# An RWKV-7 core on one core: the triangular solver's levels for two chunks issued head by head in turn, the odd chunk on exchanged partition halves, removal keys ahead of the decays

## The reference, cut to what matters

```
def step(state, inp):
    r_t, w_t, k_t, v_t, kk_t, a_t = inp
    sa = jnp.einsum('bhvk,bhk->bhv', state, kk_t)
    state = (state * w_t[:, :, None, :]
             - sa[..., None] * (kk_t * a_t)[:, :, None, :]
             + v_t[..., None] * k_t[:, :, None, :])
    return state, jnp.einsum('bhvk,bhk->bhv', state, r_t)
```

## Time and profile before

| | us |
|---|---|
| median of 3 runs | 2342.1 (2340.4 to 2342.15) |
| time of the profiled execution | 2340.44 |
| its span, first to last instruction | 2338.4 |
| TensorE busy | 2235.1 (96% of the span) |
| VectorE busy | 1552.6 (66%) |
| ScalarE busy | 1210.3 (52%) |
| mean granted TensorE clock | 0.987 |

### The profile page before, as it was taken

How to read it: one execution, slowest core, us unless ns; L and a number is a source line. 1 busy time by engine, 2 the same in 40 slices (tenths; PEclk the granted TensorE clock), 3 DMA queues, 4 the chain that set the end, 5 groups by cost and what they waited for, 6 DMA issues and landing times. The chain is left out here.

```text
span 2338.4 us, 55662 instructions
## 1 busy us (share of the span) xinstructions
PE 2235.1 (96%) x23008; PEld 2146.5 (92%) x23008; DVE 1552.6 (66%) x2401; ACT 1210.3 (52%) x2061; POOL 35.9 (2%) x51
## 2 busy tenths in 40 slices
PE   6899899999999999999988998999999999999998
PEld 6799899999999988899977998999998999888998
DVE  7754465566665688665587644655776777876776
ACT  5643454455544456644466434544677444776443
POOL 0000000000000010000000000000100000100000
PEclk9899999999999999999998999999999999999999
DMA  5310255543455433355433102554433555434553
GB/s 201 126 47 4 71 191 188 173 144 118 154 196 188 153 118 119 126 201 191 156 99 127 47 4 85 187 188 168 148 116 129 180 197 171 136 118 142 191 184 112
DMA packets 88435, 327.14 MB, mean 140 GB/s; under 512 B 9808, under 2 KB 9936, under 8 KB 87632
## 3 DMA queue, kind: packets, MB, share of 16 engines
q1 hardware_dynamic: 87984, 322.66, 40.9%
q0 software_dynamic: 288, 2.10, 0.3%
HBM read 323.67 MB, written 1.05 MB: 139 GB/s over the span
## 5 line engine op out<-in xcount | busy, mean ns | idle before, releaser
L2050 PE MATMUL bank<-h_split,w_split 128*128 128x256 f32 x3176 | 913.4, 288 | 22.4 <-DVE h_split L2269 8.6
L2051 PE MATMUL bank<-h_split,w_split 128*128 128x256 f32 x3176 | 898.7, 283 | 0.0
L2052 PE MATMUL bank<-h_split,w_split 128*128 128x256 f32 x3176 | 898.4, 283 | 0.0
L2238 DVE TENSOR_TENSOR w_split<-ring_a,w_split 128x1024 fp32r<-128x1024 f32 x474 | 568.1, 1224 | 192.2 <-ACT w_split L2135 190.9
L2050 PEld LDWEIGHTS bank<-h_split,w_split 128*128 128x128 f32 x3176 | 604.0, 190 | 35.0 <-DVE h_split L2269 11.3
L2051 PEld LDWEIGHTS bank<-h_split,w_split 128*128 128x128 f32 x3176 | 599.2, 189 | 1.4
L2052 PEld LDWEIGHTS bank<-h_split,w_split 128*128 128x128 f32 x3176 | 598.1, 188 | 0.0
L2135 ACT ACTIVATE w_split<-ring_a 128x1024 fp32r<-128x1024 f32 x474 | 483.5, 1049 | 47.9 <-PE bank L594 25.8
L2072 PE MATMUL bank<-act_split,d_split 128*128 128x256 f32 x1008 | 285.4, 283 | 3.8 <-DVE act_last L2330 2.4
L2073 PE MATMUL bank<-act_split,d_split 128*128 128x256 f32 x1008 | 285.2, 283 | 0.0
L2074 PE MATMUL bank<-act_split,d_split 128*128 128x256 f32 x1008 | 285.1, 283 | 0.0
(11 more groups left out here) (282 smaller groups left out, 3235.6 us busy)
## 6 DMA issues: line engine op xcount, KB each, us to landing
ring_a<-wa SPq DMA_DIRECT2D x474, 512.0 KB, 4.0
ring_d<-wd SPq DMA_DIRECT2D x132, 512.0 KB, 4.5
tab_sb<-tab SPq DMA_DIRECT2D x1, 2384.0 KB, 13.3
hT<-na POOLq DMA_DIRECT2D x2, 1024.0 KB, 5.2
xT<-x SPq DMA_DIRECT2D x1, 1024.0 KB, 4.9
out<-xT SPq DMA_DIRECT2D x1, 1024.0 KB, 3.9
vec_sb<-vec SPq DMA_DIRECT2D x1, 288.0 KB, 4.9
tab_sb<-tab SPq DMA_DIRECT2D x1, 65.0 KB, 4.6
```

Of the source, the lines that this page charges most:

```text
L2050: mm(dst, w[:, 0, ks], x[:, 0, k, :], start=(k == 0), stop=False)
L2051: mm(dst, w[:, 0, ks], x[:, 1, k, :], start=False, stop=False)
L2052: last = mm(dst, w[:, 1, ks], x[:, 0, k, :], start=False, stop=(k == KT - 1))
L2238: v.tensor_tensor(w_split[:, u % 4, 1, :], ring_a[:, u % 4, :], w_split[:, u % 4, 0, :].bitcast(f32), ALU.subtract).then_inc(s["w_lo"], 1)
```

## The change

- **Levels in pairs.** `level_product`, `level_update` and `level_turned` now take two chunks at once and issue their heads in turn: head n of the even chunk, head n of the odd one. The odd chunk's `X`, `Q`, `XT` lie on the exchanged half: where the even chunk's product reads partitions 0 to 63 and writes 0 to 63, the odd chunk's reads 0 to 63 and writes 64 to 127. The right sides of the odd chunks are exchanged too, and `solve` turns the halves back.
- **The turned update** is now a transpose of the copied `X` by the identity, behind the product of the next level; the first one of an odd chunk (`turned_zero`) is a new operation and takes the place of a VectorE operation (1119) for that chunk. The last level (`last_turned`) is as before.
- **Scores of chunks 2 and 3** are cut into eight parts on banks 6 and 7, and two parts are issued in each level of chunks 0 and 1. The four `bonus_sum` come ahead of the levels.
- **Projections.** The removal keys come at units 16 and 17, ahead of the second half of the running sums, which moves from unit 15 to unit 18; the exponentials are split in two and come behind the evacuations; group 5 of the mixes comes a unit later; the low part of unit 21 comes behind group 5. In the second layer the value gates come between the products of line 1055.

```diff
+        def score_bank(c, i):
+            return level_bank(c, i % 3) if c < 2 else B[6 + i % 2]
...
+            def other(h):
+                return slice(HD, P) if h.start == 0 else slice(0, HD)
...
+            def turned_zero(c):
                 q, t = counts(c)
+                pe.wait_ge(s["q_ready1"], 6 * q + 1)
+                if c > 2:
+                    pe.wait_ge(s["xtn_ready1"], 6 * q)
+                b = eight(level_bank(c, 2)[:, :])
+                for n, h in each_head():
+                    last = mm(b[other(h), n, :], Xc[c][h, n, :], ident_of(h), start=True, stop=True)
+                last.then_inc(s["xt_mm1"], 1)
+            def level_product(a, lv):
+                q = counts(a)[0]
+                for t in range(2):
+                    if lv == 1:
+                        pe.wait_ge(s[f"q_ready{t}"], 6 * q + 1)
+                    else:
+                        pe.wait_ge(s[f"xn_ready{t}"], 4 * q + lv - 1)
+                b0, b1 = [eight(level_bank(a + t, 0)[:, :]) for t in range(2)]
+                for n, h in each_head():
+                    even = mm(b0[h, n, :], scb[a][h, n, CH:2 * CH], Xc[a][h, n, :], start=True, stop=True)
+                    odd = mm(b1[other(h), n, :], scb[a + 1][h, n, CH:2 * CH], Xc[a + 1][h, n, :], start=True, stop=True)
+                even.then_inc(s["lx_mm0"], 1)
+                odd.then_inc(s["lx_mm1"], 1)
+            def level_update(a, lv):
+                q = counts(a)[0]
+                for t in range(2):
+                    pe.wait_ge(s[f"q_ready{t}"], 6 * q + lv + 1)
+                if lv == 1:
+                    pe.wait_ge(s["xt_ready"], q + 1)
+                else:
+                    pe.wait_ge(s["xtn_ready0"], 5 * q + lv - 1)
+                pe.wait_ge(s["xtn_ready1"], 6 * q + lv)
+                b0, b1 = [eight(level_bank(a + t, 1)[:, :]) for t in range(2)]
+                for n, h in each_head():
+                    o = other(h)
+                    even = mm(b0[h, n, :], XTc[a][h, n, :], Qc[a][h, n, :], start=True, stop=True)
+                    odd = mm(b1[h, n, :], XTc[a + 1][o, n, :], Qc[a + 1][o, n, :], start=True, stop=True)
+                even.then_inc(s["xn_mm0"], 1)
+                odd.then_inc(s["xn_mm1"], 1)
+            def level_turned(a, lv):
+                q = counts(a)[0]
+                for t in range(2):
+                    pe.wait_ge(s[f"xn_ready{t}"], 4 * q + lv)
+                b0, b1 = [eight(level_bank(a + t, 2)[:, :]) for t in range(2)]
+                for n, h in each_head():
+                    even = mm(b0[h, n, :], Xc[a][h, n, :], ident_of(h), start=True, stop=True)
+                    odd = mm(b1[other(h), n, :], Xc[a + 1][h, n, :], ident_of(h), start=True, stop=True)
+                even.then_inc(s["xt_mm0"], 1)
+                odd.then_inc(s["xt_mm1"], 1)
+            def last_turned(c):
+                q, t = counts(c)
+                pe.wait_ge(s[f"q_ready{t}"], 6 * q + 6)
+                pe.wait_ge(s[f"xtn_ready{t}"], (5 + t) * q + 4 + t)
                 b = eight(level_bank(c, 2)[:, :])
                 for n, h in each_head():
                     last = mm(b[h, n, :], Qc[c][h, n, :], XTc[c][h, n, :], start=True, stop=True)
                 last.then_inc(s[f"xt_mm{t}"], 1)
...
                 pe.wait_ge(s["rhs_ready"], 4 * r + c + 1)
-                pe.wait_ge(s[f"xtn_ready{t}"], 5 * q + 5)
+                pe.wait_ge(s[f"xtn_ready{t}"], (5 + t) * (q + 1))
                 b = eight(chain_bank(c, "r")[:, :])
                 for n, h in each_head():
-                    last = mm(b[h, n, :], XTc[c][h, n, :], rhs_[h, n, :], start=True, stop=True)
+                    g = other(h) if c % 2 else h
+                    last = mm(b[h, n, :], XTc[c][g, n, :], rhs_[g, n, :], start=True, stop=True)
                 last.then_inc(s["u_mm"], 1)
...
-            level_product(1, 0)
+            for c in (0, 1):
+                for i in range(4):
+                    score_part(c, i)
+            level_zero(0)
+            level_zero(1)
+            bonus_sum(0)
+            bonus_sum(1)
             level_product(0, 1)
-            bonus_sum(0)
-            level_product(1, 1)
-            bonus_sum(1)
+            turned_zero(1)
+            bonus_sum(2)
+            bonus_sum(3)
             for lv in range(1, 5):
-                for c in (0, 1):
-                    level_update(c, lv)
-                    if lv == 1:
-                        bonus_sum(2 + c)
-            level_update(0, 5)
-            scores(2)
-            level_update(1, 5)
-            scores(3)
+                level_update(0, lv)
+                score_part(2 + (lv - 1) // 2, (lv - 1) % 2 * 2)
+                level_product(0, lv + 1)
+                level_turned(0, lv)
+                score_part(2 + (lv - 1) // 2, (lv - 1) % 2 * 2 + 1)
+            last_turned(0)
+            last_turned(1)
             right(0)
-            level_product(2, 0)
+            level_zero(2)
+            level_zero(3)
             solve(0)
-            level_product(3, 0)
             level_product(2, 1)
             outputs_known(0)
-            level_product(3, 1)
+            turned_zero(3)
             state(0)
             level_update(2, 1)
             outputs(0)
+            level_product(2, 2)
+            level_turned(2, 1)
             right(1)
-            level_update(3, 1)
             head_mean(0)
...
@@ -744,14 +793,16 @@
                 split(13 + m)
                 if m < 4:
                     xm_hi(4, m)
-                if m in (4, 7):
-                    xm_hi(5, (m - 4) // 3)
+                evac(10 + m, 8 + m, 16 + m)
                 if m in (4, 6):
-                    decays(m // 2 - 2)
-                evac(10 + m, 8 + m, 16 + m)
-            split(21)
+                    falling(m // 2 - 2)
+                if m in (5, 7):
+                    rising(m // 2 - 2)
+                if m >= 6:
+                    xm_hi(5, m - 6)
             for p in range(2, 4):
                 xm_hi(5, p)
+            split(21)
             split(22)
             act.wait_ge(s["a_used"], u + 20)
             step.did(A(work[:, 5, :], B[1][:, 0:S], ACT.Sigmoid))
...
+            copy_turned(1, 0)
             for lv in range(1, 5):
-                for c in (0, 1):
-                    gain(2 * lv - 2 + c)
-                    level_copy(c, lv)
-                    if j == 0 and lv > 2 and c == 0:
-                        h = slice(4 * lv - 12, 4 * lv - 8)
-                        A(v_first[:, h, :].rearrange("p a b -> p (a b)"),
-                          qkv[:, 4 * lv + 4:4 * lv + 8, :].rearrange("p a b -> p (a b)"), ACT.Copy)
-            level_copy(0, 5)
-            level_copy(1, 5)
+                copy_x(0, lv)
+                copy_x(1, lv)
+                copy_turned(0, lv)
+                copy_turned(1, lv)
+                gain(2 * lv - 2)
+                gain(2 * lv - 1)
+                if j == 0 and lv > 2:
+                    h = slice(4 * lv - 12, 4 * lv - 8)
+                    A(v_first[:, h, :].rearrange("p a b -> p (a b)"),
+                      qkv[:, 4 * lv + 4:4 * lv + 8, :].rearrange("p a b -> p (a b)"), ACT.Copy)
+            copy_turned(0, 5)
+            copy_turned(1, 5)
             copy_rhs(0)
             copy_u(0)
-            level_copy(2, 1)
+            copy_turned(3, 0)
+            copy_x(2, 1)
...
             for m in range(8):
                 if m < 4:
                     mixed(4, m)
-                if m in (1, 2):
-                    for n in range(4 * m - 4, 4 * m):
+                if m == 1:
+                    for n in range(4):
                         running(n)
                 low(13 + m)
                 if m < 4:
                     mixed_low(4, m)
-                if m in (5, 6):
-                    for n in range(4 * m - 20, 4 * m - 16):
+                if m in (3, 4):
+                    for n in range(4 * m - 12, 4 * m - 8):
                         removal_key(n)
-                if m in (4, 7):
-                    mixed(5, (m - 4) // 3)
-                    mixed_low(5, (m - 4) // 3)
-            low(21)
+                if m == 5:
+                    for n in range(4, 8):
+                        running(n)
+                if m >= 6:
+                    mixed(5, m - 6)
+                    if m == 7:
+                        mixed_low(5, 0)
+            mixed_low(5, 1)
             mixed(5, 2)
             mixed(5, 3)
             mixed_low(5, 2)
             mixed_low(5, 3)
+            low(21)
             low(22)
             dve.wait_ge(s["gate_hi"], r + 1)
             v.tensor_tensor(work_r[:, 5, :], work[:, 5, :], work_r[:, 4, :].bitcast(f32), ALU.subtract)
...
             for h in range(2):
+                if j:
+                    value_gate(2 * h)
+                    value_gate(2 * h + 1)
                 ins = v.tensor_tensor(half_rows(oT, h), rows(0, h), rows(24, h), ALU.mult)
                 if h == 0:
```

(64 more changed lines are left out.)

146 lines of the change are left out of this document (66 added, 80 removed).

## The result

The changed kernel takes 2318.03 us (median of 4 runs, 2314.36 to 2318.44), the kernel before 2341.38 in the same series (2340.40 to 2342.15): ratio 0.9895, 95% interval 0.9881 to 0.991 (the medians themselves differ by 1.0%). Run again later beside other kernels it took 2316.94 (ratio 0.9903). The forecast was 2288 in a range of 2276 to 2325, so sign and range hold, and 29 of the 52 us forecast are missing. The profiled execution took 2314.36 us, its span 2312.3.

What follows compares the result with a forecast made beforehand. TensorE, busy 96% of the span, was taken as the bound. Cores 20.3 + 20.7, projections 4.6 + 8.1, less 1.3 for half clock, made 52.4 us off 2340.44: 2288 us, range 2276 to 2325.

Steps and rivals of the forecast that it cites:

- the price of a paired operation: In the core's levels: 64 MATMULs over four array quarters take 0.933 us, as 32 did before; from above 1.866.
- the walk: Step-by-step timing of three engine queues in the new order; cores 20.3 and 20.7 us shorter, good to about 1 us.
- issue becomes the bound: Rival for paired operations in the cores: a pair costs 1.4 us, giving 2310, or 1.6 us, giving 2320; 9%.
- The argument against it: Work that could queue behind a bonus sum starts no sooner, so the array, not issue, seems to set 58.3 ns.
- The floor of 25 ns between starts: Skill page's minimum between MATMUL starts; by it a pair costs 1.6 us and the time is near 2320 us.
- Quarters that share rows: Rival for paired operations: quarters sharing rows queue, a pair costs 1.866 us, giving 2334; 10%.
- nothing drains: Rival for paired operations: changing quarters drains the array, a pair costs 3.73 us, giving 2431, slower; 5%.
- first and third rivals: For paired operations: row-sharing quarters queue, 2334 us, 10%; changing quarters drains the array, 2431 us, 5%.
- The copies' waits: In levels of chunks 0 and 1: TensorE waits 0.49 us before product and next update, seven or eight times.
- The walk with pairs of 1.866 us: Same queue timing of the cores with dearer pairs: ends 3.0 us later than before in each layer.
- The projections: Work ahead of the cores: 4.6 us won in the first layer, 8.1 in the second, less 1.3 for half clock.
- 2 to 4 us a window: Half-clock windows among the gates and behind the core: each that goes or comes is worth half its work's length.

Runs made afterwards that it cites:

- own-halves kernel: Changed kernel with the odd chunk's heads kept on their own halves of the array, order, waits and instruction count unchanged: 2337.6 us, ratio 0.9994.
- full-array version: Changed kernel with heads laid out by parity, so a chunk's X is turned by four 128 x 128 products instead of sixteen 64 x 64: 2313.75 us, ratio 0.9888.
- the probe: Changed kernel with blocks of identity products put ahead of each layer's core, over four quarters or own halves: 2392.39 us with the blocks in it.
- e6_front_only: Kernel before the change with only the five hunks of the projections applied: 2327.38 us, ratio 0.9953.

## Why the prediction was right in sign and wrong in size

**The step that failed** is the price of a paired operation, 0.933 us, as the walk used it 26 times a core. As a burst it is right to 0.01 us (0.94). As a rate it is wrong: a page of two pairs that follows a stall lasts 3.3 to 4.0 us, so where pairs follow each other one costs 1.7 to 2.0 us, about as much as two single operations. The saving is real only where a page also holds work that is dear for its number of instructions, and where it is not, it comes back as a stall of 0.2 to 2.0 us. The walk had no term for this. With it, 14.2 of the 14.5 us missing in the first core and the 12 of the second are accounted for. That the time lay inside the range owes nothing to the mechanism forecast: the range had been drawn to take in the rival below.

**The rival "issue becomes the bound"** was the right one, at 9%, and its figures bracket the result: 2310 at a pair of 1.4 us, 2320 at 1.6. The argument against it failed. It looked at whether queued work starts sooner behind a bonus sum, which shows the rate inside a page; a limit that acts once in 127 MATMULs can't be seen in 32. The rows needed were there: the instruction queue's 25 pages in the 121.4 us of the core before, one per 4.9 us on average and never closer than 3.56 (3.32 once, in the turnings ahead of it). Twice the rate had never been asked for. The 26 pages of the changed core take 4.4 us each, the 22 of the full-array version 5.1.

The Trainium skill treats this in "Runtime: NRT & Kernel Launch", section "Instruction fetch mechanics": 16 KiB blocks of 256 instructions, fetched by the sequencer during the block before, the cost of the boundary "mostly hidden", since instructions are dispatched more slowly than they are filled in. The size of the block agrees (127 MATMULs and their weight loads); that it is hidden holds for 29 ns a MATMUL, but for one stall in the own-halves kernel, and fails at 14.8, where the probe lost 1.6 to 2.1 us at the boundaries shown. The floor of 25 ns between starts, which the prediction cited from the Trainium skill, does not show in a burst (14.8 ns on average). That the 2320 us worked out from it came nearest is luck: the limit is one per page and not one per MATMUL.

**Quarters that share rows** do not queue (1.9 us for 128 MATMULs in the probe), and nothing drains: the first and third rivals fall. In a burst the exchanged halves do all that they were made for.

**The copies' waits** are nearly as walked: seven in the first half of the core, 0.66 to 0.68 us from start to start and 0.95 for the one with the `v_first` copy, where the walk had 0.49 on top of some 0.05. The walk with pairs of 1.866 us met the own-halves kernel within 0.1 us in the first core and 1.4 in the second.

**The projections** hold in the first layer. The timeline of VectorE, with the keys (L1035) ahead of the sums (L1030), beside the earlier trace rows:

```profile
82.33 1.65 DVE L1035 SCALAR_TENSOR_TENSOR qkv<-qkv,vec_sb,bank 128x256 f32<-128x256 f32 x4
85.04 2.43 DVE L1030 TENSOR_TENSOR_SCAN ring_d<-tab_sb,ring_d 128x256 f32<-128x256 f32 x4
...
95.93 1.47 DVE L1020 TENSOR_TENSOR o_split<-work,o_split 128x512 fp32r<-128x512 f32 x2
```

The keys end at 83.98 (83.6 in the walk), the last low part at 97.40 (97.1), and TensorE's one wait from 75 to 125 us is 4.5 us for it (4.2). Gates start at 102.5 instead of 101.8. In the second layer the 7.1 us for the keys and the 1.5 for the value gates of the earlier trace rows are gone, but the view of 1225 to 1290 now has three waits that I had not walked, since I took the first layer's scale for the second:

```profile
PE bank L2122 <- DVE w_split L2310: 3.2, 1, 3.2
PE bank L354 <- DVE work_r L1102: 2.0, 1, 2.0
PE bank L2122 <- DVE o_split L1020: 1.6, 1, 1.6
```

From the end of the first core to the turning in the second layer it is 1028.94 us instead of 1034.04, 5.1 won where 8.1 was said; with the projections alone (`e6_front_only`) it is 2.2, for 9.2 in the first layer. Half clock lies in other places than before (at 95.4 and 109.0 us for 6.8 each, at 1170.6 for 13.7, at 1273.0 for 6.8) and moves between executions of nearly the same projections: the turning of the first layer starts at 133.9 to 135.4 us in most of them and at 130.5 to 130.7 in two. That is the 2 to 4 us a window that the prediction left open.

**Open.** In four cases in the first core the fetch of the next page began not 1.1 but 2.6 to 3.1 us after TensorE entered a page, in three of them 0.95 to 1.25 us behind the end of a wait within the page, and two of the three largest stalls followed. That a waiting instruction also holds up the request is what this looks like; no run took it apart. Nor did any run try a loop, though the trace holds the six in which 144 MATMULs a pass are repeated without a fetch.

## What to carry to other kernels

Count instructions as well as array time: where TensorE is to start MATMULs closer than about 29 ns for longer than one page of the stream, cut them at every 127 and see whether each piece still lasts 3.3 to 4 us. A trick that halves the array time of small products pays in part by itself (14 us here with the core alone) and better with fewer, larger products beside it: the full-array turning with its copies moved takes 7.5 to 10 us less than the changed kernel. And "issue" waits at even distances in the stream, in operations that have nothing in common, point to the stream and not to the operations.

## What the runs showed of the hardware

- Four quarters of the array take four 64 x 64 x 64 products at once, 14.8 ns a MATMUL in a burst of 128, at a granted clock of 1.00 (`e4_probe`).
- A burst lasts 127 or 128 MATMULs. After it, TensorE's next instruction comes 2.2 to 2.9 us after the fetch of its page began; and where a page was entered by a stall, the fetch of the next begins 1.0 us or more after that. Kept saturated, the probe runs at 28.7 ns a MATMUL, 3.46 to 4.01 us a page; the shortest page between two stalls of the changed core takes 3.31.
- No page is fetched while TensorE repeats a loop of 144 MATMULs and their weight loads, for 151 to 154 us at a time.
- With 16 columns instead of 64 a burst of 128 MATMULs takes 1.85 us, hardly less than the 1.88 with 64.
- A change between 64 x 64 and 128 x 128 products took 0.15 us from start to start in one direction and 0.2 in the other (`e5_full_turn`).
